# Holding back seven of the eleven first expert matrices until two row gathers have landed, and writing ScalarE's loop count earlier

## What is computed

```python
u2 = modulate(rmsnorm(x, norm_ffn_g[l]), sh_ffn, sc_ffn)
# route: sigmoid scores over 32 experts in 8 groups, best group by its top two, top two experts in it
e_idx, gw = route(uf, w_router, router_bias)
order = jnp.argsort(e_idx.reshape(A))          # tokens sorted by expert, padded to blocks
...
xb = uf[buf_tok].reshape(n_blocks, MOE_BLOCK, D)
def expert_block(args):
    xblk, e = args
    h = jax.nn.silu(xblk @ w_gate[e]) * (xblk @ w_up[e])
    return h @ w_down[e]
...
y = jax.ops.segment_sum(yb * buf_w[:, None].astype(yb.dtype), buf_tok, num_segments=N)
x = x + gt_ffn[:, None, :] * y
return rmsnorm(x, final_g)
```

## Time and profile before

| | us |
|---|---|
| median of 3 runs | 1596.37 |
| the 3 runs | 1595.51, 1596.37, 1598.94 |
| the profiled execution | 1595.06 |
| its span, of which the profile tells | 1593.2 |

### The profile page before, as it was taken

How to read it: one execution, slowest core, us unless ns; L and a number is a source line. 1 busy time by engine, 2 the same in 40 slices (tenths; PEclk the granted TensorE clock), 3 DMA queues, 4 the chain that set the end, 5 groups by cost and what they waited for, 6 DMA issues and landing times.

```text
span 1593.2 us, 32383 instructions
## 1 busy us (share of the span) xinstructions
PE 1423.9 (89%) x12413; PEld 1063.8 (67%) x12413; DVE 856.2 (54%) x1274; ACT 452.2 (28%) x972; POOL 590.7 (37%) x360
## 2 busy tenths in 40 slices
PE   4899999999999999999999799479599788879974
PEld 3677787777778887778888688356366455546641
DVE  4655544655573334445221845657467545657766
ACT  5455553444471112101101312122122111212223
POOL 2422224333244332332331211056456535546640
PEclk9899999999999999999999899589889888989996
DMA  9510003222105333343121621799999999998997
GB/s 346 148 39 26 27 27 100 75 71 77 54 24 152 105 101 105 117 158 99 40 60 52 223 85 79 295 385 421 424 424 422 422 424 423 423 424 357 423 413 280
DMA packets 122112, 332.64 MB, mean 209 GB/s; under 512 B 14208, under 2 KB 82544, under 8 KB 109744
## 3 DMA queue, kind: packets, MB, share of 16 engines
q1 hardware_dynamic: 105008, 297.11, 48.1%
q10 hardware_dynamic: 9248, 17.58, 3.5%
q0 software_dynamic: 7776, 16.84, 2.7%
HBM read 311.41 MB, written 24.00 MB: 211 GB/s over the span
## 4 chain that ended last, share of the span: by engine, by line
PE 73%; DMA 11%; DVE 9%; ACT 3%; issue 1%; SPq 1%; another core or an unknown queue 1%; DVEq 0%; ACTq 0%; POOLq 0%
PE ps L820 29%; PE ps L1076 14%; DMA w_exp<-in_w_exp_up 8%; PE ps L989 8%; PE ps L1086 6%; PE ps L1013 4%; PE ps L884 2%; PE ps L857 2%; PE ps L910 1%; PE ps L948 1%; PE ps L959 1%; DMA y<-d_y 1%; DMA ada_g<-in_ada_w 1%; PE ps L1022 1%
## 5 line engine op out<-in xcount | busy, mean ns | idle before, releaser
L1076 PE MATMUL ps<-w_exp,xT 128*32 128x256 f32 x4992 | 308.2, 401 | 75.6 <-DMA w_exp<-in_w_exp_up 40.8
L1076 PEld LDWEIGHTS ps<-w_exp,xT 128*32 128x32 f32 x4992 | 193.7, 115 | 183.6 <-issue 125.1
L820 PE MATMUL ps<-u_hi,w_hi 128*128 128x512 f32 x768 | 308.2, 401 | 6.6 <-DVE u_lo L1492 6.4
L820 PE MATMUL ps<-u_hi,w_lo 128*128 128x512 f32 x768 | 299.9, 390 | 0.0
L820 PE MATMUL ps<-u_lo,w_hi 128*128 128x512 f32 x768 | 299.5, 390 | 0.0
L739 POOL DMA_INDIRECT xg<-d_u,tok_cur x80 | 200.4, 2505 | 236.2 <-ACT tok_cur L1365 227.0
L632 POOL CAST w_hi<-w_raw 128x1024 fp32r<-128x1024 f32 x48 | 61.1, 1273 | 384.3 <-PE ps L820 210.7
L1849 DVE COPY w_down<-w_exp 128x4096 f32<-128x4096 f32 x78 | 175.7, 2252 | 0.0
L820 PEld LDWEIGHTS ps<-u_hi,w_hi 128*128 128x128 f32 x768 | 144.7, 188 | 45.9 <-issue 9.7
L820 PEld LDWEIGHTS ps<-u_hi,w_lo 128*128 128x128 f32 x768 | 144.4, 188 | 31.0
L820 PEld LDWEIGHTS ps<-u_lo,w_hi 128*128 128x128 f32 x768 | 144.7, 188 | 29.2 <-issue 1.0
(11 more groups left out here) (280 smaller groups left out, 1953.4 us busy)
## 6 DMA issues: line engine op xcount, KB each, us to landing
w_exp<-in_w_exp_gate SPq DMA_DIRECT2D x32, 2048.0 KB, 37.7
w_exp<-in_w_exp_up SPq DMA_DIRECT2D x32, 2048.0 KB, 42.9
w_exp<-in_w_exp_down SPq DMA_DIRECT2D x32, 2048.0 KB, 39.2
ada_g<-in_ada_w ACTq DMA_DIRECT2D x32, 512.0 KB, 3.7
w_raw<-in_w_in SPq DMA_DIRECT2D x24, 512.0 KB, 4.1
w_raw<-in_w_branch_gate SPq DMA_DIRECT2D x24, 512.0 KB, 4.1
bias<-d_table SPq DMA_DIRECT2D x48, 192.0 KB
ada<-in_ada_w SPq DMA_DIRECT2D x4, 2048.0 KB, 21.1
```

Source lines behind the costliest of these rows:

```text
L820: ins = pe.matmul(ps[:, 5 + h, :], a[par][:, kc, :], b[:, kc, HF[h]], start=(n == 1), stop=(n == MM))
L1076: last = pe.matmul(ps[CAP * n:CAP * (n + 1), 2, 0:QT].rearrange("p (c m) -> p c m", c=2), xT[:, CAP * kc:CAP * (kc + 1)], cols[:, n % 2], ...
```

## The change

Two things are changed, besides the numbering of lines (those behind the first piece stand 3 lines lower, behind the last one 4).

- SyncE issues the gate matrix of expert 1 after u2_ready, as before, and then waits until both first gathers (ld_xg[0] and ld_xg[1], 16 each) have landed. Only then does it issue that expert's up and down matrices and all that stands behind.
- The number of rounds (starts, index NE + 2) is written by VectorE before its wait for the list products and not behind the last reduction; it increments half_hits to 3, and ScalarE waits for that. slots_ready, for which SyncE waits too, is incremented at the old place by itself.

```diff
             sp.wait_ge(u2_ready, TT)
-            for w in "gud":
+            load_expert(1, "g")
+            for h in range(2):
+                sp.wait_ge(ld_xg[h], 16)
+            for w in "ud":
                 load_expert(1, w)
             sp.wait_ge(st_rows, 32 * TT)
...
-            sc.wait_ge(slots_ready, 2)
+            sc.wait_ge(half_hits, 3)
             rounds = sc.value_load(starts[0:1, NE + 2:NE + 3], min_val=NE // 2 - 1, max_val=NBLK // 2 - 2)
...
             ch.sync()
+            dve.tensor_scalar(starts[:, NE + 2:NE + 3], starts[:, NE + 1:NE + 2], 2.0, None, SUB).then_inc(half_hits, 1)
             dve.wait_ge(list_ps, 1)
...
-            dve.tensor_scalar(starts[:, NE + 2:NE + 3], starts[:, NE + 1:NE + 2], 2.0, None, SUB).then_inc(slots_ready, 1)
+            dve.sem_inc(slots_ready, 1)
```

## The result

Over 17 runs of each, the changed kernel took 1601.93 us (median), the kernel before 1597.79. The ratio is 1.0031, 95% interval 1.0019 to 1.0044: 5.0 us slower (3.0 to 7.0), where 4.2 was predicted. The ratio is not the quotient of the two medians, which lie 4.1 us apart. The profiled execution of the changed kernel has a span of 1600.9 us against 1593.2.

The account below looks back on a forecast made before the run. The weight stream was taken to bound the kernel: a new 7.4 us hole less the old 3.2 gives 4.2 us slower, 1599.3 against the profiled 1595.06, plus 1.3 for the median: 1600.6 us, range 1596.8 to 1604.5.

Parts of the forecast that it names:

- What bounds the stage: Expert stage: weight arrival at TensorE's last long wait (1421 us) plus a fixed run sets the end; holes move it one-for-one.
- ScalarE's number: Start of the gathers: ScalarE reads the number of rounds early and starts its first row-number copy 2.6 us earlier.
- When four matrices run dry: At SyncE's hold: the four issued matrices and small loads, 9.70 MB, leave the DMA engines empty at 1031.0 us.
- The landing: First gathers on empty engines: each lands in 3.3 us (bounds 2.7 and 7.7), the second at 1037.25 us.
- The rival of the slow gathers: First gathers take about 7 us even on an empty chip; net 8 to 9 us slower, 1605 us; chance 0.11.
- The sum: Weight stream: new hole of 7.4 us less the closed old hole of 3.2 us, net 4.2 us slower.
- The restart: Weight stream after the hold: acts like a full-rate start 1.7 us behind the issue (bounds 1.2 and 2.2).
- TensorE sets the end: Expert stage: TensorE, not the stream, sets the end, so its 6 us earlier start counts: 1590.4 us; chance 0.06.
- Cheap hold: Landing and restart near their lower bounds, or a slightly faster early stream: 0 to 3 us slower, 1596.4 to 1599.5; chance 0.20.
- a microsecond of TensorE's before 1143 us moves nothing: TensorE's early expert work: time gained or lost there has no effect, being followed by 11.4 us of waiting for weights.
- the remark that the first part, left alone, would have nothing to show: If the hold proved empty, only ScalarE's earlier number would be left, with no gain; that case had chance 0.01.
- What the profile would show: Signs: first copy near 1031.3, hole 1031 to 1039, none near 1070, first block near 1037, last long wait ending near 1425.4.

Follow-up runs that it names:

- e1: The early number alone (VectorE's and ScalarE's edits, SyncE's loads as before), against the kernel before: ratio 0.9983.
- e7: The kernel before with twelve small unused copies on ScalarE ahead of the first copy of row numbers, against the kernel before: ratio 1.0032.
- e12: The early number alone, timed once more on another chip, against the kernel before: ratio 0.9988.

## Why the prediction was right, and where not

- **What bounds the stage: right.** The last long wait ends where the stream says, and the end of the span follows it at a fixed distance in all fourteen profiles.
- **ScalarE's number: right in size.** 2.6 us earlier was expected, 2.75 measured, and 3.3 in the second profile of the changed kernel, where rows_of was ready 0.6 us sooner.
- **When four matrices run dry: right.** 1031.0 us on the clock of before is R + 22.3. The bytes fell to 166 and 51 GB/s in the two microseconds from R + 21.8.
- **The landing: a term a little too large.** 3.3 us were taken for a gather, from the loads of 64 and 256 KB; it was 2.9 from GpSimd's start to SyncE's next issue, for which the prediction had 3.4 with its 0.1 for the wait. The 2.3 us of the Trainium skill ("DMA: Bandwidth & Descriptors", "Anatomy of one DMA — SWDGE (gpsimd) path") are 0.6 below what this trace shows up to the waiting engine's start. The rival of the slow gathers, 7 us on empty engines, fell.
- **The sum: 4.2 us, of which the trace shows 3.6 by the holes (6.8 - 3.2) and 3.15 by the last long wait.** The new hole was put at 7.4 and measured 6.8; the fifth load was issued at R + 27.9, where R + 28.6 was expected, 0.5 of it from the landing and 0.15 from ScalarE. The restart was put at 1.7 us and measured 1.8. The timings say 5.0 with an interval that holds all of these; that the forecast of 4.2 lies between the traces (2.3 and 3.3 by the two spans) and the timings is no proof of it to the microsecond.
- **The rivals.** "TensorE sets the end" is out: the first block started 6.2 us earlier and the end came 3.3 us later. "Cheap hold" was to decide when the second gather landed before 1036.2 us; it landed near R + 27.8, 1036.5 on the clock of before, so the case was nearer than its place in the text suggests.
- **A step that failed:** "a microsecond of TensorE's before 1143 us moves nothing", and with it the remark that the first part, left alone, would have nothing to show. The same text had the twelfth load waiting for TensorE's buffer and the hole that comes of it; it closed that hole in the sum of both parts but did not ask what the first part would do without the second. By e1 and e7 TensorE's start counts nearly one for one until that hole is closed. The forecast did not suffer, since with the hold in place the hole is gone anyway.
- **What the profile would show:** all but one came as said, the last long wait's end 1.1 us ahead of the 1425.4 given for it (R + 415.6 is 1424.3 on the clock of before). TensorE's first long wait did not grow from 11.4 to 21 us; the time went into an earlier one (5.63 us before 1101.99) and smaller ones. The waits up to there add up to 19.7 us, 7.1 more than before (12.6), and the blocks behind a wait ran slower: 5.97 us instead of 3.66 for 64 matmuls.

## What to carry to other kernels

- In a stage that is a stream of loads into a ring of buffers, make a ledger of the holes in the stream, with what ends each one; an edit is worth what it does to the holes. Ask for each part of an edit by itself whether it moves the event that ends one.
- An engine that later waits for data can still be on the path, by the buffer that it gives back before that wait. "It waits afterwards anyway" is an argument only if the stream has no hole in between.
- Clearing the way for a small urgent transfer pays only if the big ones were going to run dry then, or can be started earlier; compare two profiles from the last event that both have in common, not from their start.

## What the runs showed of the hardware that was not expected

A gather of 128 rows of 1 KB was in the reader's hands 2.96 us after GpSimd's start on empty engines, 7.16 us with weights queued for tens of microseconds, and hardly quicker where the weights ran out only 5 us behind that start (behind five matrices: 8.1 us from ScalarE's copy, against 4.1 on empty engines); where they ran out 1.5 us behind it (weights first, hold behind six), it was 5.5. The stream did not come back at full rate from an issue on an empty queue: in the changed kernel the issue at 1041.12 was followed by 262, 262, 393 and 369 GB/s in the microseconds from 1042. With the gathers in it this is 1.29 MB by 1046, as if full rate had begun 1.8 us behind the issue. And TensorE's block after each long wait took 5 to 6.5 us instead of 3.66. In the kernel before it had stood for 11.3 us ahead of 1421.17; the granted clock of the next 6.2 us has a mean of 0.58, most of it at the lower level of 1.2 GHz (0.5), and is 1.0 (2.4 GHz) behind them (rows of before):

```profile
1421.17:1427.40 6.23, 6.23 (x68) 3.41 (x72) 0.00 (x0) 0.00 (x0) 0.00 (x0) 0.58 1.01 429
1427.40:1431.00 3.60, 3.60 (x72) 2.31 (x68) 2.83 (x6) 1.39 (x5) 1.46 (x1) 1.00 1.01 428
```

Most of the scatter of this kernel's times lies in the first 1010 us, before the stage that was changed: code that is the same up to there reached r_score at 1008.73 us in one profile (before) and at 1019.37 in another (e12). Behind it, pairs of executions of one kernel differ by 0.05, 0.9 and 1.1 us.
